# RWKV front: ScalarE copies the gate's banks between the second and the third root of the key lengths

## The chip, the cores and the metric

The kernel runs on one core of one Trainium2 chip. The metric is the device time of one execution in microseconds, as the median of timed runs. A profiled execution gives the trace; its times are counted from the start of its span. The engines are named by their work: PE is TensorE (matmul), DVE is VectorE, ACT is ScalarE, POOL is GpSimd, SP is SyncE, which issues the large loads.

## What is computed

Two layers over 256 tokens of width 1024, in float32. Layer 0 mixes tokens with HGRN2 and Mamba-2 head groups, layer 1 with RWKV-7; each mixer is followed by a mixture of 16 experts. The change is in layer 1, in front of the RWKV recurrence. What matters of it:

```python
xx = jnp.pad(h[:, :-1], ((0, 0), (1, 0), (0, 0))) - h
mixed = h[None] + xx[None] * mu[:, None, None, :]
r, k, v = jnp.einsum('ibsd,ide->ibse', mixed[:3], w_rkv)
xw, xa, xg = mixed[3], mixed[4], mixed[5]
...
a = jax.nn.sigmoid((a0 + (xa @ a1) @ a2).astype(f32))
g = jax.nn.sigmoid(xg @ g1) @ g2
...
kk = heads(k * k_k)
kk = kk / jnp.maximum(jnp.sqrt(jnp.sum(kk * kk, axis=-1, keepdims=True)), 1e-12)
...
o = rwkv7_scan(r_h, w_h, k_h, v_h, kk, a_h)
...
o = (o.reshape(bsz, s_len, d) * g).astype(h.dtype)
```

The gate g is needed only at the very end, where it multiplies the output of the recurrence. The normalized keys kk are needed at once: the recurrence is solved in blocks of 128 tokens, and the matrix of the first solve is a product of keys.

## The kernel before

Every engine has its own program, written out by hand in the order in which it runs. An engine does one instruction after the other and stops where it has to wait for a semaphore; what stands behind a waiting instruction waits with it. There is no scheduler.

Activations are held transposed: 8 blocks of 128 features by 256 tokens. A projection with transposed output (L784, in project_T) takes one weight tile of 512 output columns in two halves; each half fills one bank of PSUM, 128 x 512, with 16 matmuls (the trace shows 32 records for them). Banks 0 to 3 go round: proj_bank gives the next of them, and where a bank was used before, TensorE waits until proj_evac says that its last content was copied out. So the n-th use of a projection bank waits for the (n - 4)-th copy. Banks 4 to 7 are used by hand.

In the front of the RWKV layer TensorE does, in this order: the low-rank products of decay, rate and gate; the key projection, two tiles (L784); the sums of squared keys over each head, key_lengths (L1261), four times, into banks 4 to 7; the gate's second product, gate_second (L1239), into four projection banks; then rkv(1, 0), the first tile of the receptance projection, whose first half (L784) wants the bank that holds the first quarter of the gate. Between its two halves stand the first two of four key products (L1275, into banks 4 to 7, which wait for a_ready of DVE and for all four key maxima, kk_max), behind it the other two, then the second receptance tile, the value projection (L795), and the solve (from L1356 on).

DVE reads the sums of squares out of banks 4 to 7: key_max(u) (L2406) takes the larger of the sum and 1e-24 into rinv[u % 2]. There are only two buffers rinv, so the order is: key_max 0 and 1; key_scale 0 and 1 (L2413, L2414), which multiply the keys by the inverse root; key_first 0 and 1 (L2418), which write the operand of the key products and raise a_ready; then key_max 2 and 3; then scale and first for 2 and 3; then L2433, a product over a whole buffer. Later it masks the copied products (L2440) and inverts the diagonal blocks.

ScalarE does the roots: key_root(u) is one Ln (L1610) and one Exp (L1616) on rinv[u % 2], after key_max(u). The gate's four banks are copied to SBUF by evac_T, through L1633 in evacuate, which raises proj_evac. Behind these come evac_products (L1829), the copies of the key products; L1846, an exponential over a buffer that GpSimd writes with L729; and the copies of the receptance banks (L1633). GpSimd starts L729 when all four a_ready are there.

SyncE loads the weights. The six tiles of the three projections are loaded through line L509; each load waits until its slot in the ring is free, and the last one, the second half of the value weights, waits for gate_second.

Of the kernel before, what the change touches and what calls it, by code (L numbers as in the profile page):

```python
# [104 lines left out]
def trunk(nc, t, out):  # L105
# [31 lines left out]
    with ExitStack() as ctx:  # L137
# [339 lines left out]
        def norm_total(k):  # L477

            return bank[6][:, 0:S] if k else bank[4][:, S:2 * S]
        COND = sum(g == 1 for g, _, _ in VEC.values())  # L480

        block = ctx.enter_context(nc.Block())
# [3 lines left out]
        def _(sp):  # L486
# [57 lines left out]
            for l in range((NSUB + 1) // 2):  # L544
                base = M[l]
                for n, (tile, slot, _) in enumerate(plan[l]):
                    if n >= SLOTS:

                        if tile[0] == "wo":
                            continue  # L550
                        wait_used(l, n - SLOTS)
                    elif l == 0 and n == 2:

                        sp.wait_ge(vec_landed, 16 * (len(VEC) - COND))
                    elif l > 0 and n == 0:

                        g_end = sp.value_load(tab_i[0:1, NE - 1:NE], min_val=1, max_val=NE)
                        sp.wait_ge(M[l - 1]["w3_done"], g_end)
                    elif l > 0 and n == 2:

                        sp.wait_ge(M[l - 1]["down_half"], g_end * 2)
                    elif l > 0 and n == 4:

                        g_end = sp.value_load(tab_i[0:1, NE:NE + 1], min_val=NE // 2, max_val=NE)
                        sp.wait_ge(M[l - 1]["w1_done"], g_end)
                    load(tile, slot)
                    if l == 0 and n == SLOTS - 1:
                        load_small()
# [70 lines left out]
        def _(pool):  # L639
# [74 lines left out]
            expert_norm(1)  # L714

            _, slot, count = plan[1][places[1, "la"][0]]
            pool.wait_ge(tile_landed[slot], 16 * count)
            for i in range(2):
# [826 lines left out]
        def _(act):  # L1545
# [63 lines left out]
            def logarithm(dst, src, scale, bias):  # L1609
                act.activation(dst, src, ACT.Ln, bias=bias, scale=scale).then_inc(stat_ln, 1)  # L1610

            def inverse_roots(dsts, first):

                for u, dst in enumerate(dsts):
                    act.wait_ge(stat_ln, first + u + 1)
                    act.activation(dst, dst, ACT.Exp, scale=-0.5).then_inc(stat_rstd, 1)  # L1616
# [12 lines left out]
            def evacuate(dst, func=ACT.Copy, **kw):  # L1629

                n = evac[0]
                act.wait_ge(proj_full, n + 1)
                act.activation(dst, bank[n % 4][:], func, **kw).then_inc(proj_evac, 1)  # L1633
                evac[0] += 1

            def evac_T(dst, first, func=ACT.Copy):
                for u in range(2):
                    b = first + 2 * u
                    evacuate(dst[:, b:b + 2, :].rearrange("p k s -> p (k s)"), func)
# [137 lines left out]
            if NSUB >= 3:  # L1777
# [25 lines left out]
                def evac_keys(u):  # L1803

                    n = evac[0]
                    act.wait_ge(proj_full, n + 1)
                    act.activation(k1T[:, 2 * u:2 * u + 2, :].rearrange("p k s -> p (k s)"), bank[n % 4][:], ACT.Copy)
                    if u == 0:
                        act.wait_ge(keys_ready, 1)
                    for c in range(2):  # L1810
                        b = 2 * u + c
                        act.activation(kkT[:, b, :], bank[n % 4][:, c * S:(c + 1) * S], ACT.Copy,
                                       scale=col("od_k_k", b))
                        ins = act.activation(blocks(5)[:, b, :], bank[n % 4][:, c * S:(c + 1) * S], ACT.Square,
                                             scale=col("od_k_k", b))
                    ins.then_inc(proj_evac, 1)
                    evac[0] += 1

                def key_root(u):
                    act.wait_ge(kk_max, u + 1)  # L1820
                    logarithm(rinv[u % 2], rinv[u % 2], 1.0, 0.0)
                    inverse_roots([rinv[u % 2]], 5 + u)

                def evac_products(j):

                    act.wait_ge(lt_full, j + 1)
                    for hh in range(2):
                        dst = LT[:, 8 * j:8 * j + 8, :].rearrange("p (v h) s -> p v h s", h=2)[:, :, hh, :]
                        ins = act.activation(dst, bank[4 + 2 * (j % 2) + hh][:].rearrange("p (v s) -> p v s", v=4),  # L1829
                                             ACT.Copy, scale=-1.0)  # L1830
                    ins.then_inc(lt_evac, 1)
# [4 lines left out]

                for u in range(4):
                    evac_keys(u)
                for u in range(4):
                    key_root(u)  # L1840
                evac_T(ggT, 0)
                evac_T(ggT, 4)
                for j in range(4):
                    evac_products(j)
                act.wait_ge(rw_diff, 4)
# [734 lines left out]
```

## Time and profile before

| | before |
|---|---|
| median of 3 timed runs | 1210.8 us (1210.73 to 1210.84) |
| the profiled execution | 1203.89 us |
| its span, first to last instruction | 1202.2 us |
| TensorE busy | 1144.8 us (95%) |
| VectorE busy | 418.5 us (35%) |
| ScalarE busy | 266.6 us (22%) |
| GpSimd busy | 90.7 us (8%) |
| mean granted TensorE clock | 0.972 |
| read from HBM | 307.55 MB, 257 GB/s over the span |

TensorE is busy nearly all the time, and the other engines a third of it or less. A share of 95% leaves 57 us in which TensorE stood, and it says nothing of how fast TensorE ran while it was busy: for that there is the granted clock, 1.00 for 2.4 GHz and 0.50 for 1.2 GHz. The stretch of the change is from 733 to 770 us of the span.

### The profile page before, as it was taken

What the parts mean: (1) busy time and instruction counts of PE and PEld (TensorE: products, weight loads), DVE (VectorE), ACT (ScalarE), POOL (GpSimd) and SP (SyncE); (2) the same over time, 40 slices, a digit from 0 to 9 for tenths busy, and PEclk for the clock granted to TensorE, in tenths of its full rate; (3) what the DMA queues carried; (4) which work ended last, traced back from release to release, by engine and by line L of the source; (5) the groups of instructions that cost most, each with busy time, mean ns of one, the idle gap of its engine ahead of it and who ended that gap; (6) DMA issues with size and microseconds to landing.
All of it is one profiled execution on the core that took longest, in us unless ns stands there. A gap on an engine that the chain in (4) does not pass through costs nothing.

```text
span 1202.2 us, 15755 instructions
## 1 busy us (share of the span) xinstructions
PE 1144.8 (95%) x6555; PEld 758.4 (63%) x6555; DVE 418.5 (35%) x932; ACT 266.6 (22%) x439; POOL 90.7 (8%) x120
## 2 busy tenths in 40 slices
PE   5899999998989999999999897999989999999997
PEld 3686798984478844444444576848878744444454
DVE  0364853365720321111111485565432411111113
ACT  2222110414220311111111344233230311111112
POOL 5002221200000100000000102111000100000000
PEclk9899999999989899999999998999989899999998
DMA  9797774439967379959999712000069599999991
GB/s 351 264 340 279 280 271 149 141 129 370 402 236 262 119 291 387 386 217 349 389 386 338 286 71 70 1 0 2 7 261 387 186 335 387 387 386 386 386 382 42
DMA packets 157180, 309.56 MB, mean 258 GB/s; under 512 B 9568, under 2 KB 10940, under 8 KB 157116
## 3 DMA queue, kind: packets, MB, share of 16 engines
q1 hardware_dynamic: 156320, 307.39, 70.3%
q8 instruction: 51, 0.84, 0.3%
q10 hardware_dynamic: 796, 1.23, 0.3%
q14 instruction: 13, 0.11, 0.0%
HBM read 307.55 MB, written 1.05 MB: 257 GB/s over the span
## 4 chain that ended last, share of the span: by engine, by line
PE 90%; DVE 3%; SPq 3%; ACT 2%; DMA 1%; issue 1%; ACTq 1%; DVEq 0%
PE bank L1141 19%; PE bank L784 16%; PE bank L1165 10%; PE bank L845 7%; PE bank L1074 7%; PE bank L1066 6%; PE bank L795 5%; PE bank L911 2%; PE bank L817 1%; PE bank L754 1%; PE bank L1427 1%; SPq L509 1%; PE bank L1417 1%; PE bank L1335 1%; DMA ring<-in_ev_w_in 1%
## 5 line engine op out<-in xcount | busy, mean ns | idle before, releaser
L784 PE MATMUL bank<-arena,ring 128*128 128x256 f32 x960 | 216.2, 387 | 10.4 <-ACT arena L1633 6.3
L784 PEld LDWEIGHTS bank<-arena,ring 128*128 128x128 f32 x960 | 185.6, 195 | 37.7 <-issue 9.9
L1141 PE MATMUL bank<-ring,arena 128*64 128x512 f32 x704 | 153.7, 592 | 0.0
L1141 PEld LDWEIGHTS bank<-ring,arena 128*64 128x64 f32 x704 | 50.4, 137 | 99.6 <-issue 99.4
L2328 DVE TENSOR_TENSOR arena<-arena,bank 128x512 f32<-128x512 f32 x17 | 11.7, 687 | 220.7 <-PE bank L1141 220.7
L845 PE MATMUL bank<-arena,ring 128*128 128x256 f32 x384 | 85.4, 386 | 2.9 <-DVE arena L2551 2.9
L1074 PE MATMUL bank<-arena 128*128 128x256 f32 x336 | 84.2, 398 | 1.7 <-issue 1.7
L1141 PE MATMUL bank<-arena 128*64 128x512 f32 x384 | 84.1, 592 | 0.0
L845 PEld LDWEIGHTS bank<-arena,ring 128*128 128x128 f32 x384 | 74.4, 194 | 13.7 <-issue 3.2
L1066 PEld LDWEIGHTS bank<-arena 128*128 128x128 f32 x608 | 69.3, 192 | 13.8 <-issue 13.8
L1066 PE MATMUL bank<-arena 128*128 128x128 f32 x608 | 72.7, 278 | 0.0
L1074 PEld LDWEIGHTS bank<-arena 128*128 128x128 f32 x336 | 64.6, 202 | 11.6 <-issue 3.4
L1165 PE MATMUL bank<-ring,arena 128*64 128x512 f32 x288 | 63.8, 595 | 0.0
L1141 PEld LDWEIGHTS bank<-arena 128*64 128x64 f32 x384 | 27.6, 137 | 54.8 <-issue 54.8
L1165 PE MATMUL bank<-arena 128*64 128x512 f32 x256 | 56.7, 595 | 0.0
L795 PE MATMUL bank<-ring,arena 128*128 128x512 f32 x128 | 55.5, 592 | 0.0
L2344 DVE COPY arena<-bank 128x512 f32<-128x512 f32 x17 | 11.8, 692 | 102.3 <-PE bank L1165 102.3
L1165 PEld LDWEIGHTS bank<-ring,arena 128*64 128x64 f32 x288 | 19.9, 137 | 39.0 <-issue 39.0
L1971 DVE SCALAR_TENSOR_TENSOR arena<-ring,csilu,arena 128x512 f32<-128x512 f32 x56 | 43.6, 779 | 2.0
L1752 ACT ACTIVATE arena<-bank 128x512 f32<-128x512 f32 x19 | 11.3, 597 | 142.5 <-PE bank L1066 142.5
L795 PEld LDWEIGHTS bank<-ring,arena 128*128 128x128 f32 x128 | 24.2, 190 | 29.3 <-issue 29.2
L1762 ACT ACTIVATE arena<-bank 128x512 f32<-128x512 f32 x17 | 10.1, 597 | 139.5 <-PE bank L1141 139.5
(366 smaller groups left out, 1302.7 us busy)
## 6 DMA issues: line engine op xcount, KB each, us to landing
ring<-in_moe_w SPq DMA_DIRECT2D x112, 1024.0 KB, 14.2
arena<-in_moe_w SPq DMA_DIRECT2D x80, 1024.0 KB, 14.3
ring<-in_mod_w SPq DMA_DIRECT2D x24, 2048.0 KB, 11.1
ring<-in_ev_w_in SPq DMA_DIRECT2D x13, 2048.0 KB, 13.1
ring<-in_od_w_rkv SPq DMA_DIRECT2D x6, 2048.0 KB, 13.5
ring<-in_ev_w_out SPq DMA_DIRECT2D x4, 2048.0 KB, 17.3
ring<-in_od_w_o SPq DMA_DIRECT2D x2, 2048.0 KB, 10.5
arena<-in_x ACTq DMA_DIRECT2D x1, 1024.0 KB, 9.1
```

What stands on the lines that cost most here:

```text
L509: sp.dma_start(dst, src).then_inc(tile_landed[slot], 16)
L754: mm = pe.matmul(norm_total(k), ones[:, 0:P], squares[:, b, :], start=(b == 0), stop=(b == KB - 1))
L784: mm = pe.matmul(ps[:, c * S:(c + 1) * S], w_cols(slot)[:, k, (2 * half + c) * P:(2 * half + c + 1) * P], src[:, k, :], start=(k == 0), st ...
L795: mm = pe.matmul(ps[:, :], src[:, k, tt * P:(tt + 1) * P], w_cols(slot)[:, k, :], start=(k == 0), stop=(k == KB - 1))
L817: mm = pe.matmul(row_bank[32 * c:32 * (c + 1), :], slide[g][:, k, 31 - i:63 - i], w_cols(slot)[:, k, :], start=(m == a and r == 0), stop=( ...
L845: mm = pe.matmul(bank[d // 2][:, (d % 2) * S:(d % 2 + 1) * S], w_rows(slot)[:, kk, d * P:(d + 1) * P], srcs(4 * j + kk), start=(j == 0 and ...
L911: mm = pe.matmul(ps[:, hh * 64:(hh + 1) * 64], et, right, start=True, stop=True)
L1066: mm = pe.matmul(bank[6 + kb // 4][:, (kb % 4) * P:(kb % 4 + 1) * P], hN[:, tt, kb * P:(kb + 1) * P], pick[:, tt, :], start=(tt == 0), sto ...
L1074: mm = pe.matmul(bank[d // 2][:, (d % 2) * S:(d % 2 + 1) * S], ymoe[:, d * P:(d + 1) * P], spread, start=(first and d % 2 == 0), stop=last ...
L1141: mm = pe.matmul(bank[4 + half][e * C:(e + 1) * C, :], hgT[:, kb, e * C:(e + 1) * C], piece(slots[e], kb), start=(kb == 0), stop=(kb == KB ...
L1165: mm = pe.matmul(bank[5 + half][e * C:(e + 1) * C, :], hidT[:, f, e * C:(e + 1) * C], piece(slots[e], 4 * half + f), start=(f == 0), stop= ...
L1971: ins = stt(acc, w_cols(slot)[:, k, :], csilu[:, k:k + 1], acc, ALU.mult, ALU.add)
```

## The change

Before, ScalarE takes the four key roots one after the other and then copies the gate's four banks. Now the four copies stand between the second and the third root. Nothing else is edited.

```diff
                 for u in range(4):
                     evac_keys(u)
-                for u in range(4):
-                    key_root(u)
+                key_root(0)
+                key_root(1)
                 evac_T(ggT, 0)
                 evac_T(ggT, 4)
+                key_root(2)
+                key_root(3)
                 for j in range(4):
                     evac_products(j)
```

ScalarE's program, behind the second root. L1610 and L1616 are a root's Ln and Exp, L1633 the copy of a gate bank, L1829 the copy of a key product. Lines with a minus stand only before, those with a plus only after:

```order
+L1633 ACTIVATE arena<-bank2 128x512 [waits proj_full]
+L1633 ACTIVATE arena<-bank3 128x512 [waits proj_full]
+L1633 ACTIVATE arena<-bank0 128x512 [waits proj_full]
+L1633 ACTIVATE arena<-bank1 128x512 [waits proj_full]
 L1610 ACTIVATE arena<-arena 128x512 [waits kk_max]
 L1616 ACTIVATE arena<-arena 128x512 [waits stat_ln]
 L1610 ACTIVATE arena<-arena 128x512 [waits kk_max]
 L1616 ACTIVATE arena<-arena 128x512 [waits stat_ln]
-L1633 ACTIVATE arena<-bank2 128x512 [waits proj_full]
-L1633 ACTIVATE arena<-bank3 128x512 [waits proj_full]
-L1633 ACTIVATE arena<-bank0 128x512 [waits proj_full]
-L1633 ACTIVATE arena<-bank1 128x512 [waits proj_full]
```

Four copies moved ahead of four root instructions, the first of which waits for DVE (kk_max). The two programs have the same number of instructions, and no load of activation tables comes in.

TensorE's program at the same place, which is the same before and after: the sums of squares, the gate, then the receptance tile in two halves with key products in and behind it, the second receptance tile, and the values:

```order
L1261 MATMUL bank<-arena,same_head 128x256 x8
L1239 MATMUL bank<-scratch,ring 128x256 x8
L784 MATMUL bank<-arena,ring 128x256 x16
L1275 MATMUL bank<-arena 128x128 x16
L784 MATMUL bank<-arena,ring 128x256 x16
L1275 MATMUL bank<-arena 128x128 x16
L784 MATMUL bank<-arena,ring 128x256 x32
L795 MATMUL bank<-ring,arena 128x512 x32
```

Nothing moved here. The first L784 behind L1239 is the instruction that waits for the copy of bank 2.

## Rows read from the trace of the kernel before

**Rows 1.** The page, part 4: the chain that ended last, by engine.
```profile
PE 90%; DVE 3%; SPq 3%; ACT 2%; DMA 1%; issue 1%; ACTq 1%; DVEq 0%
```

**Rows 2.** TensorE's waits: who waited for whom, us in total, times, longest us.
```profile
PE bank L784 <- ACT arena L1633: 6.3, 1, 6.3
```

**Rows 3.** Time line of TensorE: start us, us, what, records [idle before <- releaser].
```profile
736.33 3.62 PE L1239 MATMUL bank<-scratch,ring 128*128 128x256 f32 x16
746.20 10.20 PE L784 MATMUL bank<-arena,ring 128*128 128x256 f32 x32 [6.25 <-ACT arena L1633]
756.32 2.06 PE L1275 MATMUL bank<-arena 64*128 64x128 f32 x32
758.31 7.17 PE L784 MATMUL bank<-arena,ring 128*128 128x256 f32 x32
...
781.31 27.63 PE L795 MATMUL bank<-ring,arena 128*128 128x512 f32 x64
```

**Rows 4.** Time line of ScalarE, from the second root on.
```profile
738.93 0.63 ACT L1616 ACTIVATE arena<-arena 128x512 f32<-128x512 f32 x1
743.10 0.63 ACT L1610 ACTIVATE arena<-arena 128x512 f32<-128x512 f32 x1 [3.53 <-DVE arena L2406]
...
744.94 0.63 ACT L1616 ACTIVATE arena<-arena 128x512 f32<-128x512 f32 x1
745.47 2.04 ACT L1633 ACTIVATE arena<-bank 128x512 f32<-128x512 f32 x4
757.53 2.06 ACT L1829 ACTIVATE ring<-bank 128x512 f32<-128x512 f32 x4 [10.02 <-PE bank L1275]
...
768.54 1.93 ACT L1846 ACTIVATE arena<-arena 128x2048 f32<-128x2048 f32 x1
770.34 1.11 ACT L1633 ACTIVATE arena<-bank 128x512 f32<-128x512 f32 x2
```

**Rows 5.** Time line of DVE in the same stretch.
```profile
741.18 1.28 DVE L2418 TENSOR_TENSOR arena<-arena 128x512 f32<-128x512 f32 x2
742.38 1.28 DVE L2406 TENSOR_SCALAR arena<-bank 128x512 f32<-128x512 f32 x2
...
748.35 2.28 DVE L2433 TENSOR_TENSOR arena<-arena 128x2048 f32<-128x2048 f32 x1
758.72 3.42 DVE L2440 TENSOR_TENSOR arena<-ring,strict 32x256 f32<-32x256 f32 x8 [8.08 <-ACT ring L1829]
```

**Rows 6.** Windows: us, busy PE, PEld, DVE, ACT, POOL, granted clock, DMA share, GB/s.
```profile
736.00:739.90 3.90, 3.90 (x19) 3.13 (x17) 2.97 (x6) 2.41 (x4) 0.61 (x1) 1.00 0.00 0
...
740.90:741.90 1.00, 0.00 (x0) 0.00 (x0) 1.00 (x3) 0.00 (x0) 0.00 (x0) 1.00 0.77 59
741.90:742.90 1.00, 0.00 (x0) 0.00 (x0) 1.00 (x2) 0.00 (x0) 0.00 (x0) 0.61 1.02 387
...
748.00:750.00 2.00, 2.00 (x6) 1.60 (x5) 2.00 (x2) 0.00 (x0) 1.48 (x1) 0.50 0.00 0
```

**Rows 7.** Windows further on: a short stop, a slow spell, the last expert layer.
```profile
808.00:809.70 1.70, 0.97 (x5) 0.17 (x4) 0.00 (x0) 0.60 (x1) 0.66 (x2) 1.00 0.00 0
...
876.00:878.00 2.00, 2.00 (x11) 2.00 (x11) 0.21 (x2) 0.00 (x0) 0.00 (x0) 0.50 1.04 391
...
1000.00:1050.00 50.00, 50.00 (x264) 24.69 (x264) 8.71 (x23) 7.34 (x10) 0.00 (x0) 1.00 1.05 387
```

**Rows 8.** Time lines of TensorE and ScalarE at the start of the solve.
```profile
809.68 0.69 PE L1356 MATMUL bank<-arena,ring 32*32 32x32 f32 x32 [0.73 <-issue]
...
801.89 1.06 ACT L1857 ACTIVATE arena<-arena 32x1024 f32<-32x1024 f32 x1
```

**Rows 9.** GpSimd: line L729 (ns min/median/max), then the memset behind it.
```profile
L729 POOL TENSOR_TENSOR arena<-arena x2: 1912/2900/3889, 748.5 to 752.4; 128x1024 f32<-128x1024 f32 x2
...
754.22 1.80 POOL L732 MEMSET arena<- 128x2048 f32 x1
```

**Rows 10.** Time line of SyncE's DMA queue: the last load of the projections.
```profile
739.98 0.37 SPq L509 DMA_DIRECT2D ring<-in_od_w_rkv  x1
```

## The prediction

> **What bounds the kernel now.** I read four views in this order. First the chain that ended last, by engine [rows 1]: TensorE holds 90% of it, so almost only what stops or slows TensorE counts. Then TensorE's waits [rows 2]: one of them names exactly the instructions that the change moves. L784, the matmul of a transposed projection, waited once for L1633, the ScalarE copy of a gate bank, for 6.3 us. Then the time line of each engine around it, to see who was free and when [rows 3 to 5]. Last the windows, for TensorE's granted clock on both sides of the stop [rows 6, 7].
>
> TensorE's line reads as follows [rows 3]. The gate's second product (L1239) runs from 736.33 for 3.62 us, so to 739.95. Then nothing until 746.20, 6.25 us later, when the first half of the receptance projection starts. It takes 10.20 us for 32 records. The second half, the same 32 records, takes 7.17 us. So this wait has two prices: the stop itself, and a slow start after it. The windows give the reason for the second [rows 6]: the granted clock is 1.00 (2.4 GHz) up to 741.9, that is for two microseconds after TensorE has stopped, is down at some point of the next microsecond (0.61), and is 0.50 (1.2 GHz) while TensorE works at 748 to 750. A half without such a start is the second one.
>
> Why was the bank so late? ScalarE's line [rows 4]: the second key root ends its last instruction, started at 738.93, and then ScalarE stands for 3.53 us, until 743.10, for the third root's input. That input is DVE's key maximum (L2406), which starts at 742.38 because DVE has the scaling of the first keys and two products (L2418, to 742.46) ahead of it [rows 5]. Behind the fourth root, whose last instruction starts at 744.94, the four gate copies start at 745.47. TensorE starts 0.73 us after the first of them. The copies had long been possible: all four gate banks were written by 739.95. They stood in ScalarE's queue behind two roots that waited for DVE, and DVE has nothing to do with the gate.
>
> **The change, part by part.** Four ACTIVATEs of L1633 go ahead of the third root; nothing is added or removed, and TensorE's and DVE's orders stay.
>
> 1. The first copy. In the trace of before, it starts 0.53 us after the start of the root instruction ahead of it (744.94 to 745.47) [rows 4]. After the second root that makes 738.93 + 0.53 = 739.46. Its bank is the first of the four that L1239 fills, a quarter of 3.62 us into the run from 736.33, so it is full by about 737.3. TensorE follows 0.73 us after the start of the copy: 740.19. It ended L1239 at 739.95, so it stands 0.24 us instead of 6.25. Gain 746.20 - 740.19 = 6.01 us.
>
> 2. The clock. With 0.24 us of standing I expect no fall: in the trace the level held for two microseconds of standing [rows 6], and a stop of 0.73 us at 808.94 (before 809.68 [rows 8]) left it at 1.00 [rows 7]. Then the first half runs as the second did: 10.20 - 7.17 = 3.03 us. The bounds of this term are 0 (the clock falls all the same) and 3.03; I take 3.03, because both rows that are near it, a two-microsecond stand and a short stop, show a full clock.
>
> 3. The other three copies and the third root. The four took 2.04 us in all [rows 4]. From 739.46 on they end by 741.5: the fourth gate bank is written at 739.95, before the turn of its copy comes three quarters through. The third root can't start before 743.10 whatever ScalarE does, since its input comes from DVE. The margin is 1.6 us, in ScalarE's old idle time: cost 0. If the cover were gone and the roots came later, TensorE would notice only at the fifth step.
>
> 4. What is late next: the first key products. TensorE would be through the first half at 740.19 + 7.1 = 747.3, and then wants the second a_ready and the fourth key maximum. DVE gives them at 742.46 and 743.7 [rows 5], in an order that the change leaves alone. Margin 3.6 us, cost 0.
>
> 5. The third and fourth key products. TensorE wants them at 747.3 + 2.0 + 7.1 = 756.4. Their inputs are complete when DVE starts L2433 at 748.35 [rows 5]. Margin 8 us, cost 0. Their banks need the first products' copies: L1829 starts 1.2 us after TensorE starts L1275 (756.32 to 757.53) [rows 3, 4], so at 748.5, when ScalarE has been free since 745.6. Cost 0.
>
> 6. The stream that follows. ScalarE's next large instruction waits for GpSimd: L1846 exponentiates what L729 wrote. Before, GpSimd was through L729 by 754.22 [rows 9] and ScalarE came at 768.54 [rows 4]; after, ScalarE comes 9.0 us earlier, at about 759.5. L729 itself can get slower: its two instructions took 3889 and 1912 ns [rows 9], and the slow one ran while DVE ran L2433, an operation with two inputs (748.35 to 750.63 [rows 5]). DVE's first eight masked products (L2440, two inputs too), which came at 758.72, 3.42 us of them [rows 5], now come from about 750.7 on and so beside GpSimd's second instruction. If they stop GpSimd altogether, L729 ends at 754.2 + 3.4 = 757.6. Margin 1.9 us to ScalarE, and behind it 10 us more: the receptance copies came at 770.34 [rows 4], and TensorE starts the value projection, which wants their banks, at 781.31 [rows 3]. Cost 0.
> The Trainium skill ("GPSIMD Engine Reference", specifications) says that GpSimd shares its SBUF interfaces with VectorE and contends with instructions that have two SBUF inputs. By that rule, the trace agrees: 3889 against 1912 ns. It would change the sum only if the delay passed the margins.
>
> 7. The rest of the layer. The inversion on DVE starts from the fourth products' copy and moves with TensorE; ScalarE takes its last result from 801.89 on, for 1.06 us, and TensorE comes to L1356 at 809.68 [rows 8]. Both sides move alike, so the 6 us of margin stays. The weights: nothing was on the DMA rings at 736 to 739.9 [rows 6], and the sixth and last load of the three projections is issued at 739.98 [rows 10], when L1239 is done, before as after. So everything but the second half of the value weights had landed; that one is read 40 us later. The loads of the last expert layer are released by TensorE's progress and move along.
>
> Sum: 6.01 + 3.03 = 9.0 us. The profiled execution took 1203.89 us with a span of 1202.2; it would become 1194.9. The median of the timed runs is 1210.8, which is 6.9 us longer; where these are spent the profile can't show. The difference is applied to it unchanged: 1201.8 us.
>
> **The rivals.**
> - *Only the stop goes* (6.0 us, 1204.8). The clock falls in spite of the short stand, or the timed runs didn't have this slow start. For: the profiled execution isn't one of the timed ones. Against: step 2's rows.
> - *Later slow starts land differently.* The stream behind 740 moves by 9 us, and the clock falls again in it: 0.50 at 876 to 878 with TensorE busy [rows 7]. One such spell costs about as much as the one that goes, 3.0 us. If one grows or shrinks by two thirds, the gain is 7 or 11 us: 1203.8 or 1199.8.
> The Trainium skill ("TensorE: Matmul & The Clock Gate", section on the HAM clock gate) calls the moment of the change run-variable, not tied to the kernel's start. Against it stands that the timed runs here lie within 0.11 us of each other; no single trace can decide it.
> - *Another wait takes its place* (0 us, 1210.8). TensorE's wait before L784 is for three things: the bank, the weights and the mixed input. Had one of the others been only just in time, the stop would stay. Against: the weights had landed by 736 (step 7), and the mixed input is written by DVE ahead of everything that rows 5 show of it, the step before the scans of the decay.
> - *Slower: the unbroken run is paid back.* TensorE now goes from the key projection through to the solve with no stop over a microsecond. If the chip answered that with the lower level, every microsecond of work at it would cost half a microsecond. It would have to hold for 18 us to eat 9.0; at 25 us the kernel would be at 1210.8 - 9.0 + 12.5 = 1214.3. Against: at 1000 to 1050 TensorE is busy for 50.00 of 50 us at a clock of 1.00 [rows 7].
>
> **How the numbers follow.** The forecast, both terms and nothing later, has 0.78. Only the stop 0.09, later spells moved 0.08, another wait 0.03, slower 0.02. The likeliest time is 1201.8. The range runs from 1199.8 (a later spell mostly gone) to 1204.8 (only the stop). What a measurement of this kernel can tell from no change is about 0.2%, 2.4 us. Forecast, only the stop and moved spells are all beyond it: 0.95 faster; 0.03 the same; 0.02 slower.
>
> **What would show it.** In the profile of after: TensorE's wait for L1633 before L784 under 0.5 us; the first half of L784 behind it in about 7.1 us and a clock of 1.00 at 740 to 757; the third root still starting at 743.1, released by DVE; L1829 first at 748.5; L1356 at about 800.7. A third root at a later time than 743.1 would refute step 3, a wait before L1275 step 4 or 5, a wait of L1848 for GpSimd step 6. The prediction is wrong if TensorE's new start is near 746 or the clock reads 0.50 after 740.

## The result: 1199.9 us, and 9.05 us less in the stretch of the change

| | before | after |
|---|---|---|
| median of the timed runs | 1210.82 us (1210.73 to 1211.87) | 1199.88 us (1197.77 to 1200.89) |
| ratio, with its 95% interval | 1 | 0.9905 (0.9888 to 0.9923) |
| the profiled execution | 1203.89 us | 1200.02 us |
| its span | 1202.2 us | 1198.3 us |

Forecast were 1201.8 us and a range of 1199.8 to 1204.8. The kernel got faster, as forecast, but by 10.9 us in place of 9.0. The ratio of 0.9905, applied to the 1210.8 us that the forecast started from, gives 1199.3 us, half a microsecond under the range. And the two profiled executions differ by only 3.9 us. Three numbers for one change, 9.0, 10.9 and 3.9, are what has to be explained.

First the place itself. TensorE's waits of after, which answer to [rows 2]:

```profile
PE bank L784 <- ACT arena L1633: 0.2, 1, 0.2
```

TensorE's time line of after, against [rows 3] (start us, us, what, records, idle before and who ended it):

```profile
741.28 3.62 PE L1239 MATMUL bank<-scratch,ring 128*128 128x256 f32 x16
745.15 7.14 PE L784 MATMUL bank<-arena,ring 128*128 128x256 f32 x32 [0.25 <-ACT arena L1633]
752.23 2.06 PE L1275 MATMUL bank<-arena 64*128 64x128 f32 x32
754.21 7.17 PE L784 MATMUL bank<-arena,ring 128*128 128x256 f32 x32
...
777.22 27.63 PE L795 MATMUL bank<-ring,arena 128*128 128x512 f32 x64
```

The stop of 6.25 us is 0.25 (forecast 0.24), the first half takes 7.14 us in place of 10.20 (forecast 7.17), and nothing new stands between it and the value projection. The granted clock is the third number from the right, in windows over the same stretch (compare [rows 6]):

```profile
745.00:747.00 2.00, 1.85 (x9) 1.67 (x10) 1.97 (x4) 1.48 (x4) 0.00 (x0) 1.00 0.20 60
747.00:750.00 3.00, 3.00 (x16) 2.64 (x15) 2.17 (x4) 1.88 (x4) 0.00 (x0) 1.00 1.04 391
```

It is 1.00 in both, and in the windows behind them to 777 us. ScalarE and DVE, against [rows 4] and [rows 5]:

```profile
743.89 0.63 ACT L1616 ACTIVATE arena<-arena 128x512 f32<-128x512 f32 x1
744.43 2.05 ACT L1633 ACTIVATE arena<-bank 128x512 f32<-128x512 f32 x4
748.05 0.63 ACT L1610 ACTIVATE arena<-arena 128x512 f32<-128x512 f32 x1 [1.58 <-DVE arena L2408]
```
```profile
747.33 1.28 DVE L2408 TENSOR_SCALAR arena<-bank 128x512 f32<-128x512 f32 x2
753.31 2.28 DVE L2435 TENSOR_TENSOR arena<-arena 128x2048 f32<-128x2048 f32 x1
755.63 6.74 DVE L2442 TENSOR_TENSOR arena<-ring,strict 32x256 f32<-32x256 f32 x8
```

The four copies fill what was ScalarE's idle time, and the third root still waits 1.58 us for DVE behind them: step 3's margin of 1.6 us. (The lines of DVE and of ScalarE behind the edit are numbered two higher than before: L2408 was L2406, L2435 was L2433, L2442 was L2440.) One line is not as it was: the first eight masked products of DVE take 6.74 us, where they took 3.42.

But all these times are 4.95 us later than in the trace of before: L1261, the sums ahead of the gate, starts at 732.88 there and at 737.83 here. No code ahead of it has changed. So I cut each trace into three parts: from the start to L1261, from L1261 to L1356 (the front, where the edit is), and from L1356 to the end.

| trace | start to L1261 | L1261 to L1356 | L1356 to end |
|---|---|---|---|
| before | 732.9 | 76.80 | 392.5 |
| after | 737.8 | 67.75 | 392.7 |

In the middle part, 9.05 us are gone: 6.00 of the stop, 3.05 of the slow start. The forecast was 9.04. The rest is the other two parts, and it took experiments to learn what they do.

### The profile page after: what moved, and what is told of

It is laid out like the page before. It is cut to its first block, busy times and chain, and to the rows that moved or that the text cites. A ratio compares the mean times of both kernels' runs of the same rounds, so it can differ in the third digit from the quotient of the medians.

```text
span 1198.3 us, 15755 instructions
## 1 busy us (share of the span) xinstructions
PE 1146.2 (96%) x6555; PEld 758.6 (63%) x6555; DVE 422.2 (35%) x932; ACT 266.6 (22%) x439; POOL 90.9 (8%) x120
## 4 chain that ended last, share of the span: by engine, by line
PE 90%; DVE 3%; SPq 3%; ACT 2%; DMA 1%; issue 1%; ACTq 1%; DVEq 0%
PE bank L1141 20%; PE bank L784 16%; PE bank L1165 10%; PE bank L845 7%; PE bank L1074 7%; PE bank L1066 6%; PE bank L795 5%; PE bank L911 2%; PE bank L817 1%; PE bank L754 1%; PE bank L1427 1%; SPq L509 1%; PE bank L1417 1%; DMA ring<-in_ev_w_in 1%; PE bank L1335 1%
## 5 line engine op out<-in xcount | busy, mean ns | idle before, releaser
L784 PE MATMUL bank<-arena,ring 128*128 128x256 f32 x960 | 212.9, 383 | 4.8 <-ACT arena L1600 2.7
L784 PEld LDWEIGHTS bank<-arena,ring 128*128 128x128 f32 x960 | 183.3, 192 | 31.1 <-issue 3.9
L845 PE MATMUL bank<-arena,ring 128*128 128x256 f32 x384 | 85.6, 386 | 2.9 <-DVE arena L2553 2.9
L845 PEld LDWEIGHTS bank<-arena,ring 128*128 128x128 f32 x384 | 74.6, 194 | 13.8 <-issue 3.2
L795 PE MATMUL bank<-ring,arena 128*128 128x512 f32 x128 | 57.8, 613 | 0.0
L795 PEld LDWEIGHTS bank<-ring,arena 128*128 128x128 f32 x128 | 25.2, 198 | 30.7 <-issue 30.6
```

The costliest lines, as they stand in the source:

```text
L784: mm = pe.matmul(ps[:, c * S:(c + 1) * S], w_cols(slot)[:, k, (2 * half + c) * P:(2 * half + c + 1) * P], src[:, k, :], start=(k == 0), st ...
L795: mm = pe.matmul(ps[:, :], src[:, k, tt * P:(tt + 1) * P], w_cols(slot)[:, k, :], start=(k == 0), stop=(k == KB - 1))
L845: mm = pe.matmul(bank[d // 2][:, (d % 2) * S:(d % 2 + 1) * S], w_rows(slot)[:, kk, d * P:(d + 1) * P], srcs(4 * j + kk), start=(j == 0 and ...
```

## The experiments

**The control.** The kernel of before, with no edit. It tells how far two executions of one kernel differ, and where.

> The kernel of before, unchanged, once more: a control. Its profiled execution took 1203.9 us and its timed runs 1210.8; the profile of after entered the stretch of the change 4.95 us later than that of before, in code that is the same. Theory: the granted clock falls at some stops of TensorE in one execution and not in another, ahead of the change. Then the ratio to the kernel before is 1.000, the spans of its executions differ among each other by 3 to 7 us, and what differs lies ahead of 733 us: from the first L2361 behind the key projection to the end stays at 469.1 us (+-1). Rival: the profiled execution of before was on a chip that is a little faster throughout; then every execution here agrees with the others within 0.5 us.

Twelve executions took 1204.20 to 1213.42 us, with a median of 1210.74; the ratio is 1.0008 (0.9986 to 1.0031). The traced one has a span of 1211.5 us, 9.3 more than the trace of before. Its parts are 742.3, 76.78 and 392.5 us: the whole difference lies ahead of L1261. The rival, a chip that is faster throughout, is out, and the spread is larger than the 3 to 7 us expected. The executions of before that ran beside the experiments, and these twelve, are 79 with the first four: 1203.95 to 1215.92 us, mean 1209.8, median 1210.1, standard deviation 3.4.

The largest piece shows at TensorE's stop ahead of L911. In the trace of before the 32 records behind it are quick:

```profile
117.79 3.76 PE L911 MATMUL bank<-arena 128*128 128x64 f32 x32 [2.09 <-DVE arena L2063]
121.39 13.95 PE L795 MATMUL bank<-ring,arena 128*128 128x512 f32 x32
```

In the control the same stop, 2.09 us too, is followed by a slow one:

```profile
119.89 6.97 PE L911 MATMUL bank<-arena 128*128 128x64 f32 x32 [2.09 <-DVE arena L2063]
```

and the windows of the control have the clock at 1.00 during the stop and at 0.50 behind it:

```profile
118.00:120.00 2.00, 0.11 (x1) 0.14 (x2) 1.97 (x3) 0.00 (x0) 0.00 (x0) 1.00 0.00 0
120.00:123.00 3.00, 3.00 (x15) 3.00 (x16) 2.86 (x5) 0.00 (x0) 0.00 (x0) 0.50 0.00 0
```

Of the 9.4 us ahead of L1261, L911 is 3.2, and the L795 behind it 1.8 (15.72 us in place of 13.95). A later spell is 2.4: the 64 records of L784 from 224.31 on took 16.45 us, with the clock at 0.50 from 223 to 229, and in the trace of before 14.03 us at 1.00. Another piece is a load: TensorE waited for the first weights (L784 for in_ev_w_in) 1.3 us in the trace of before and 4.6 in the control, 3.3 more. Smaller pieces of both signs make -1.3. So the theory holds for most of the difference; the wait for the load was not in it.

**The change once more.** The kernel of after, with no edit, on the chip of the control.

> The change itself once more, beside the control. Theory (stop and slow start both gone, 9.0 us, and nothing else): the ratio is 0.9925, and from the mixing step behind the key projection to the end it takes 460.3 us against 469.1. If the 10.9 us of the first measurement were a gain of the change, the ratio is 0.9905 again and the stretch behind the change is shorter by 11.

Median 1199.89 us (1198.91 to 1203.43), ratio 0.9941 (0.9918 to 0.9965). The middle part is 67.75 us again, to the hundredth. From L1261 to the end it took 458.75 us, 1.7 less than in the first trace of the change: the last part was 391.0 here against 392.7. That is the second rival of the prediction, seen in a trace: a later slow spell of TensorE was shorter. In the first trace the clock was 0.50 in the windows from 871.6 to 878.3 us, in this one from 874.5 to 877.8. The measured ratio is neither of the two expected ones; the 0.9925 of the theory lies in its interval, and the first measurement's 0.9905 does not.

**The copies still earlier,** between the first and the second root.

> The four gate copies already between the first and the second root. The theory says that TensorE's start is all that counts and that DVE's key maxima have 3.6 us of margin: the second root comes 2.2 us later, DVE's fourth key maximum about 2 us later, still 1.4 us before TensorE wants it; the remaining 0.24 us stop before L784 goes. So the same as the change, or 0.2 us faster (ratio to before 0.9923). Rival: the roots are what matters; then it is about 2 us slower than the change (0.994).

```diff
                 key_root(0)
-                key_root(1)
                 evac_T(ggT, 0)
                 evac_T(ggT, 4)
+                key_root(1)
                 key_root(2)
```

TensorE doesn't stop at all:

```profile
744.09 3.62 PE L1239 MATMUL bank<-scratch,ring 128*128 128x256 f32 x16
747.54 7.07 PE L784 MATMUL bank<-arena,ring 128*128 128x256 f32 x32
754.54 2.06 PE L1275 MATMUL bank<-arena 64*128 64x128 f32 x32
```

The middle part is 67.27 us, 0.5 under the change. L2435 starts 17.5 us behind L1261, against 15.5 with the change: DVE was made 2.0 us late, as expected, and TensorE didn't notice: the fourth key maximum ended at 753.44, 1.1 us before L1275. The margin of step 4 is real. Timed, the kernel (1199.67) can't be told from the change (1199.89).

**The copies later,** between the third and the fourth root.

> The four gate copies between the third and the fourth root. The first copy starts at the fourth root's old place, 744.29 in the times of the trace of before, so TensorE starts at 745.02, 1.18 us before the old start, after a stop of 5.1 us. The theory says that the clock has fallen by then (it fell 2 to 3 us into the stop), so the slow first half of 10.2 us stays: a gain of 1.2 us, ratio 0.9990. If the gain came from somewhere else than the length of TensorE's stop, for example from the copies no longer standing beside DVE's work, it would be near the change's 9 us.

```diff
                 key_root(1)
+                key_root(2)
                 evac_T(ggT, 0)
                 evac_T(ggT, 4)
-                key_root(2)
                 key_root(3)
```

```profile
745.69 3.62 PE L1239 MATMUL bank<-scratch,ring 128*128 128x256 f32 x16
754.38 9.05 PE L784 MATMUL bank<-arena,ring 128*128 128x256 f32 x32 [5.08 <-ACT arena L1633]
```

The stop is 5.08 us, 1.17 less than before, as worked out. The slow start stayed, but it cost 1.1 us less than expected (9.05 against 10.20 us), so the middle part is 74.49 us, 2.3 under before. The clock came back sooner: it is 0.94 in the window from 758 to 760 us, some 4 to 6 us behind the start of the first half, and in the trace of before it was still 0.50 from 750 to 752, as far behind that start. One trace doesn't show whether that is the work of the shorter stop. Median 1208.05, ratio 0.9994 (0.9971 to 1.0016), which holds both 1.2 and 2.3 us. The place of the copies decides: on the other side of one root, 7 of the 9 us are lost.

**Only the slow start.** The order of before, and TensorE kept busy through the stop. The 13 matmuls multiply two constant tiles; their result is used by nothing.

> The order of before, with 13 more matmuls of two constant tiles behind the gate's second product (into bank 4, whose sums DVE has read by then; their result is overwritten and used by nothing). They keep TensorE busy for about 5.9 us of the 6.2 us stop. The theory has two terms, 6.0 us for the stop and 3.0 for the slow start: here the stop stays and only the slow start can go. So the first half of the receptance projection takes 7.1 us in place of 9.7 to 10.2, and the kernel is 2.5 to 3 us faster than before (ratio 0.9977). Rival: the slow first half has another cause, for example the copies and DVE's work beside it; then it stays at about 10 us and nothing is gained.

```diff
                 gate_second()
+                pe.wait_ge(kk_max, 2)
+                for n in range(13):
+                    pe.matmul(bank[4][:, 0:S], same_head[:], ones[:, 0:S], start=True, stop=True)
                 pe.wait_ge(mix_ready, 6)
```

```profile
743.70 3.62 PE L1239 MATMUL bank<-scratch,ring 128*128 128x256 f32 x16
747.15 5.78 PE L1304 MATMUL bank<-ones,same_head 128*128 128x256 f32 x26
753.57 7.14 PE L784 MATMUL bank<-arena,ring 128*128 128x256 f32 x32 [0.65 <-ACT arena L1636]
```

The first half starts 9.87 us behind the start of L1239, as before, and then takes 7.14 us. The middle part is 73.76 us: 3.04 under before. The two terms of the sum are thus measured apart. Timed, 1207.56 us, ratio 0.9983 (0.9963 to 1.0003); 0.9977 was expected, and the interval just reaches no change. The timing alone doesn't show a gain; the trace shows where 3.04 us went.

**Only two of the four copies moved.**

> Only the first two gate banks are copied between the second and the third root; the other two behind the fourth. TensorE needs bank 2 for the first half and bank 3 for the second; banks 0 and 1 only for the next receptance tile, some 14 us after the first half starts, when the copies behind the roots are long done. By the theory the whole gain stays: the stop 0.25 us, the first half 7.1 us, from the key lengths to the end 460 us as with the change. Rival: the third and fourth copy matter; then TensorE waits before the second receptance tile.

```diff
                 evac_T(ggT, 0)
-                evac_T(ggT, 4)
                 key_root(2)
                 key_root(3)
+                evac_T(ggT, 4)
```

Stop 0.25 us, first half 7.14 us, middle part 67.75 us, the last part 392.7: from L1261 on 460.4, as expected. Two copies are enough. Timed 1202.84 (1197.37 to 1205.54), ratio 0.9926 (0.9896 to 0.9955).

**DVE's slow products.** GpSimd starts L729 later.

> The change, with one more wait: GpSimd starts L729 only after the third pair of key product copies, so not beside DVE's first eight masked products. These took 6.74 us in the profile of after, 3.42 in that of before. If GpSimd's L729 at the same time is the cause, they take 3.4 us again. L729 then ends some 6 us later than DVE needs nothing of it and ScalarE's exponential waits for it, up to about 5 us, while TensorE has 10 us of margin there: the total stays that of the change. Rival: DVE's masked products are slow for another reason (TensorE's or ScalarE's traffic at full clock); then they stay at 6.7 us.

```diff
             pool.wait_ge(a_ready, 4)
+            pool.wait_ge(lt_evac, 3)
```

DVE's line (numbers one higher than after's):

```profile
750.91 3.42 DVE L2443 TENSOR_TENSOR arena<-ring,strict 32x256 f32<-32x256 f32 x8
758.91 6.76 DVE L2443 TENSOR_TENSOR arena<-ring,strict 32x256 f32<-32x256 f32 x8 [4.58 <-ACT ring L1830]
```

and GpSimd's:

```profile
759.03 4.13 POOL L730 TENSOR_TENSOR arena<-arena 128x1024 f32<-128x1024 f32 x2 [22.19 <-ACT ring L1830]
```

The first eight products take 3.42 us again, and now the second eight take 6.76, which is where L729 went (here L730). The slowness follows GpSimd's operation, so that is its cause. ScalarE's exponential waited 3.33 us for GpSimd, within the 5 us expected. I had overlooked that the third pair of copies is also what the second eight wait for, so the collision was moved, not removed. The middle part is 67.75 us all the same: even 3.3 us of delay right in front of the inversion were covered by the margin of step 7.

**Two more stops filled.** The early copies, and six constant matmuls in each of two later stops.

> The gate copies between the first and the second root, and besides, six matmuls of constant tiles in each of two other stops of TensorE of about 3 us: behind the sums of the norm in front of the RWKV layer, and behind the last head variance, before the output projection. Their result is used by nothing. In the trace of before, the matmuls behind these stops are slow: L1203 takes 5.07 us where L1209, the same number of the same shape, takes 3.63, and the first 128 records of L845 take 30.03 us where 128 records of L784 take 27.86. If a stop without work makes the clock fall, both go: 1.4 + 2.2 = 3.6 us faster than the kernel without the fill. Rival: the fill matmuls come too early or too late in the stop, the clock falls all the same and nothing is gained; or they delay the work behind them, at 0.45 us each.

```diff
                 norm(2)
+                for n in range(6):
+                    pe.matmul(bank[5][:, 0:S], same_head[:], ones[:, 0:S], start=True, stop=True)
...
                 head_var(3)
+                pe.wait_ge(mean_used, 4)
+                for n in range(6):
+                    pe.matmul(bank[MEAN_BANK[3]][:, 0:S], same_head[:], ones[:, 0:S], start=True, stop=True)
                 pe.wait_ge(stat_ln, 13)
```

```profile
899.75 27.86 PE L845 MATMUL bank<-arena,ring 128*128 128x256 f32 x128 [0.26 <-issue]
```

The output projection takes 27.86 us where the trace of before has 30.03, and L1203, here L1205, 3.67 where it was 5.07 (32 records each). Median 1196.10, ratio 0.9883 (0.9855 to 0.9910). Once more on another chip, beside the change:

> The filled kernel again (copies between the first and second root, six constant matmuls in each of two stops), on one chip with the change: 3.6 us for the two slow starts and 0.5 us for the early copies and what stands in the trace of it, so about 3.5 to 4 us under the change, ratio to before 0.9895. If its first measurement was luck of spread, it is level with the change.

Median 1198.19, ratio 0.9898 (0.9863 to 0.9932). The thirteen executions of both have a mean of 1197.3 us. The change beside it:

> The change a third time, as the base of the two kernels beside it. So far its executions took 1197.8 to 1203.4 us, and the kernel of before 1204.0 to 1215.3. If the change is worth 9.0 us and all else is spread, the mean of its executions stands 9 us under that of before's, which is about 1209.6: 1200.6.

Median 1200.72 (1196.86 to 1206.59), mean 1201.8, ratio 0.9932 (0.9905 to 0.9959); middle part 67.75 us for the third time. The 22 executions of the change have a mean of 1201.1 and a median of 1200.2, so the filled kernel is 3.8 us under the change by the means (two standard errors: 1.7); 3.6 and 0.5 were expected.

**The stop ahead of L911.** The filled kernel, with four more constant matmuls.

> The filled kernel with four more constant matmuls in the stop of 2.09 us that TensorE makes ahead of its first L911, at 116 us. In the trace of before the 32 records behind that stop took 3.76 us, at a clock of 1.00, in that of the control 6.97 us with the clock down. Theory: this stop is one of the places at which an execution is lucky or not, and a cause of the spread of a kernel that is the same each time. With the fill, L911 takes 3.76 us and the 32 records of L795 behind it 13.95 us in its trace, the mean of the executions falls by 1 to 4 us under the filled kernel's, and the spread gets smaller. Rival: the fall comes from the work ahead of the stop; then L911 is slow in some executions all the same.

```diff
                 h = (HALVES + [P])[i]
+                for n in range(4 if i == 0 else 0):
+                    pe.matmul(bank[7][:, 0:S], same_head[:], ones[:, 0:S], start=True, stop=True)
                 pe.wait_ge(ek_ready, i + 1)
```

```profile
115.31 1.89 PE L903 MATMUL bank<-ones,same_head 128*128 128x256 f32 x8
117.57 3.76 PE L913 MATMUL bank<-arena 128*128 128x64 f32 x32 [0.36 <-issue]
121.16 13.95 PE L795 MATMUL bank<-ring,arena 128*128 128x512 f32 x32
```

Median 1192.81 us (1187.95 to 1194.50), ratio 0.9861 (0.9821 to 0.9900), mean 1192.0: 5.3 us under the filled kernel's (two standard errors: 2.6), where 1 to 4 were expected. In the trace both groups are at their quick times. The spread did not shrink: the standard deviation of six executions is 2.8 us, that of the filled kernel's seven on the same chip 2.0. So this stop is one cause of lost time, and in 10 of the 12 traces without the fill the 32 records behind it were slow; it isn't what makes executions differ, or not alone. This is the fastest kernel of the case, 1.4% under before. The place of the gate copies gives it 9.5 us (76.80 less 67.27), and the fills the rest of the difference of the means, some 8.

## Why the prediction was right and where it was wrong

| trace | start to L1261 | L1261 to L1356 | L1356 to end | span |
|---|---|---|---|---|
| before | 732.9 | 76.80 | 392.5 | 1202.2 |
| control | 742.3 | 76.78 | 392.5 | 1211.5 |
| copies later | 742.2 | 74.49 | 391.1 | 1207.8 |
| stop filled | 740.2 | 73.76 | 392.0 | 1206.0 |
| the change | 737.8 | 67.75 | 392.7 | 1198.3 |
| the change, 2nd | 739.0 | 67.75 | 391.0 | 1197.7 |
| the change, 3rd | 743.4 | 67.75 | 392.7 | 1203.8 |
| two copies | 743.2 | 67.75 | 392.7 | 1203.6 |
| GpSimd later | 733.1 | 67.75 | 391.1 | 1192.0 |
| copies earlier | 740.6 | 67.27 | 393.2 | 1201.1 |
| filled | 740.6 | 67.27 | 390.4 | 1198.2 |
| filled, 2nd | 740.2 | 67.26 | 389.2 | 1196.7 |
| filled, L911 too | 728.6 | 67.26 | 390.3 | 1186.2 |

**Steps 1 and 2 were right** to 0.01 and 0.02 us: 6.00 and 3.05 us, and each term was seen alone, the second with the stop filled (3.04), the first in part with the later copies (1.17 of 1.18 us). The sum of 9.04 is the middle column's 9.05.

**Steps 3, 4, 5 and 7 were right:** less the 4.95 us, the third root starts at 743.10 (748.05 in its trace), L1829 at 748.48 and L1356 at 800.63, where 743.1, 748.5 and 800.7 were forecast. The margins held also where an experiment used 2.0 us of DVE's and 3.3 us of the inversion's.

**Step 6 was right in its cost and wrong in its mechanism.** I let DVE hold up GpSimd by 3.4 us. Instead L729 took nearly as long as before (5.94 us against 5.76), and DVE's eight products took 3.3 us longer. Nothing waited for them: DVE had them done at 762.37, and the next copies came at 763.64. The margin there was 1.3 us, on DVE, and the sum had only looked at ScalarE's, 1.9 us.

**What failed is the last step of the sum,** "the difference is applied to it unchanged", and with it the range. It took 1210.8 us as the time of the kernel before. Three runs within 0.11 us looked like an exact number, but the 79 executions of that kernel reach from 1204.0 to 1215.9 us, with a mean of 1209.8. I saw that the profiled execution was 6.9 us quicker, wrote that the profile can't show why, and gave that no term in the range. It was a warning that could be read: two executions of one kernel that differ by 6.9 us suggest a spread of that size. The change's 22 executions have a mean of 1201.1, so the difference of the means is 8.7 us, with an uncertainty of about 1.4 (two standard errors, from standard deviations of 3.4 and 2.8 us). That agrees with the 9.05 of the middle part. The 10.9 us of the first measurement has 1.9 us more, because 1210.8 is 1.1 us over the mean of its kernel and 1199.9 is 1.2 under that of the change. Where in the kernel these lie stays open: only one of these eight executions has a trace. Nor is it shown to be mere chance: an estimate by drawing four of the 79 at random gives four as close together as the first measurement's (1210.73 to 1211.87) less than once in a hundred, so something may have held these together that no run shows. The 3.9 us between the first two traces is 8.85 us less from L1261 on and 4.95 more ahead of it. A range with the spread of a median of four in it would have begun near 1198 and held the time: medians of four drawn from the 79 have a standard deviation of 1.9 us.

**Of the rivals,** "another wait" and "slower" are refuted by the middle column. "Only the stop goes" is refuted by the first half's 7.14 us. "Later slow starts land differently" is true as a mechanism: down to the row of the early copies the last column moves between 391.0 and 393.2 us, with the same code in it. Nothing shows that the change moves it: ahead of L1261, where the change can't reach, the same happens on a larger scale, 732.9 to 743.4 us. I used the narrow timed runs against this rival; the 79 executions speak for it. So does the stop ahead of L911, 2.09 us each time, behind which 32 records took from 3.76 us (in two traces) over 4.80 and 5.75 to 7.04 in the twelve traces without a fill there. The Trainium skill ("TensorE: Matmul & The Clock Gate", the section on the HAM clock gate) says that the number of slow matmuls of one kernel differs from run to run. These traces agree.

## What to carry to other kernels

A copy that frees a bank for TensorE belongs ahead of any instruction on its engine that waits for a third engine; read for each long wait of TensorE what stands between the releaser's input and the releaser in its queue, and count the slow start behind the stop beside the stop itself. Where a stop can't be removed, matmuls of constant tiles in it, about as long as it is, take away the slow start; the six ahead of L845 cost nothing here (it starts 91.92 us behind L1356 with them, 91.90 without). And compare two traces from a common instruction just ahead of the edit, not by their spans: the middle part repeated to 0.03 us where the whole kernel spread over 12.

## What the runs showed of the hardware

- A stop of TensorE of 2.09 us was followed by the full clock in two traces and by half the clock in ten, with the same code there. The fall need not come in the stop: in the trace of after, where L911 starts at 118.13, the clock is 1.00 up to 120.6 and 0.50 from 120.7 to 127.4, with TensorE busy. After the stops of 0.25 and 0.65 us ahead of L784 and of 0.73 us ahead of L1356 it was full every time (behind the 0.73 us: 1.00 from 809.7 to 820 in the trace of before). The first half behind a stop of 5.08 us took 9.05 us, behind 6.25 and 6.26 us 10.20 and 10.16.
- GpSimd's L729 (128 x 1024, two inputs) and DVE's L2442 (32 partitions x 256, two inputs) beside each other: the eight instructions of DVE took 6.74 us in place of 3.42, nearly all of the difference in two of them, of 2015 and 2041 ns against a median of 420. The line's own view in the trace of after (ns min/median/max):

```profile
L2442 DVE TENSOR_TENSOR arena<-ring,strict x8: 414/420/2041, 755.6 to 761.9; 32x256 f32<-32x256 f32 x8
L729 POOL TENSOR_TENSOR arena<-arena x2: 2089/2987/3885, 753.5 to 757.3; 128x1024 f32<-128x1024 f32 x2
```

  L2435, 2048 elements wide, beside the same operation was not slowed (2.28 us), and there it was GpSimd that was (3885 ns against 2089 for its second instruction). So which of the two pays differs, and the ends of the records say why: the one that is under way makes the other wait for its end. DVE's two slow products end at 757.65 and 759.70 us, each 0.28 behind the end of one of GpSimd's two instructions (757.37 and 759.42). With GpSimd later they end at 761.38 and 763.44, behind 761.11 and 763.16. The other way round, in the trace of before L2433 ends at 750.64 and GpSimd's slow instruction 1.77 us later, with 1.91 us for the next one that has no neighbour. For other instructions no run here tests it.
